# A hybrid decoder step: the order of weight splits and probabilities, and a low-rank gate block with both weight parts

## What is computed

```python
h = rms_norm(x, norm_g)
proj = h @ w_in                       # 13,840 columns, split into twelve parts
q = rope(rms_norm(a_q, q_norm_g), pos)        # 16 heads of 64
k = rope(rms_norm(a_k, k_norm_g), pos)        # 4 heads
# A: attention in a window of 128 keys, with a sink per head
m = max(max(s), sink); p = exp(s - m); p = p / (sum(p) + exp(sink - m)); o_a = p @ v
# B: trailing means over 2, 4, 8 and 16 positions, minus the token, times w_pool
# C: gated linear attention; its decay comes from a low-rank gate:
log_a = log_sigmoid(c_lr @ w_gate_lr + b_gate) / 16      # c_lr is (tokens, 16)
br = branches * silu(gate paths), each @ w_branch
y = x + (sum over branches of sigmoid(gates) * br) @ w_out
```

## Time and profile before

| what | value |
|---|---|
| median of three runs (lowest to highest) | 2330.77 us (2329.85 to 2331.12) |
| the profiled execution's own time | 2328.41 us |
| span of the profile | 2326.6 us |
| TensorE busy | 2292.4 us (99%), 15984 matmuls |
| VectorE, ScalarE, GpSimd busy | 1373.4 us (59%), 1013.4 us (44%), 71.6 us (3%) |
| mean granted TensorE clock | 0.998 |
| read from and written to HBM | 341.59 and 20.50 MB |

### The profile page before, as it was taken

One profiled execution on the slowest core, in us unless ns is written; L12 is line 12 of the kernel. 1 busy time (PEld: TensorE's weight loads), 2 busy tenths in 40 slices (PEclk: granted clock), 3 DMA queues, 4 the chain that ended last, 5 costly groups with the idle time before them and its releaser, 6 DMA issues.

```text
span 2326.6 us, 38299 instructions
## 1 busy us (share of the span) xinstructions
PE 2292.4 (99%) x15984; PEld 2248.5 (97%) x15984; DVE 1373.4 (59%) x2335; ACT 1013.4 (44%) x1816; POOL 71.6 (3%) x110
## 2 busy tenths in 40 slices
PE   8999999999999999999999999999999999999997
PEld 8999999899999999999999999988999999999997
DVE  6766866865554455446657677578654445544543
ACT  5444356654333333333343443566543333333332
POOL 0010000000000000000001001000000000000000
PEclk9999999999999999999999999999999999999999
DMA  7333653334444444445553436533344444444453
GB/s 271 134 131 130 220 203 121 100 118 150 149 152 148 154 146 153 147 154 191 193 205 126 144 129 235 179 116 103 122 150 151 148 151 149 153 147 153 158 197 118
DMA packets 97132, 360.65 MB, mean 155 GB/s; under 512 B 11376, under 2 KB 11376, under 8 KB 96128
## 3 DMA queue, kind: packets, MB, share of 16 engines
q1 hardware_dynamic: 86400, 313.82, 40.2%
q0 software_dynamic: 9840, 43.02, 5.2%
q10 hardware_dynamic: 720, 1.36, 0.2%
HBM read 341.59 MB, written 20.50 MB: 156 GB/s over the span
## 4 chain that ended last, share of the span: by engine, by line
PE 90%; DVE 5%; ACT 3%; issue 2%; DMA 0%; POOL 0%; ACTq 0%; DVEq 0%; POOLq 0%
PE main L1491 83%; PE side L1491 5%; DVE w_lo L428 1%; ACT tc L1256 1%; PE side L1495 1%; ACT w_hi L1049 1%; ACT probs L1216 0%; DVE small L767 0%; DVE q_a L443 0%; ACT tb L1068 0%; DVE probs L762 0%; DVE tc L443 0%; DVE ta L447 0%; ACT tb L1070 0%; DVE q_a L739 0%
## 5 line engine op out<-in xcount | busy, mean ns | idle before, releaser
L1491 PE MATMUL main<-xg_hi,w_hi 128*128 128x320 f32 x3488 | 1093.7, 314 | 10.1 <-DVE w_lo L428 10.1
L428 DVE TENSOR_TENSOR w_lo<-raw,w_hi 128x512 fp32r<-128x512 f32 x1192 | 790.6, 697 | 521.0 <-ACT w_hi L1049 509.4
L1491 PE MATMUL main<-xg_hi,w_lo 128*128 128x320 f32 x3488 | 1078.5, 309 | 0.0
L1491 PE MATMUL main<-xg_lo,w_hi 128*128 128x320 f32 x3488 | 1078.3, 309 | 0.0
L1049 ACT ACTIVATE w_hi<-raw 128x512 fp32r<-128x512 f32 x1192 | 714.5, 626 | 702.2 <-PE main L1491 687.7
L1491 PEld LDWEIGHTS main<-xg_hi,w_hi 128*128 128x128 f32 x3488 | 655.6, 188 | 19.2 <-DVE xg_lo L462 10.1
L1491 PEld LDWEIGHTS main<-xg_lo,w_hi 128*128 128x128 f32 x3488 | 655.7, 188 | 2.0
L1491 PEld LDWEIGHTS main<-xg_hi,w_lo 128*128 128x128 f32 x3488 | 655.4, 188 | 0.0
L1491 PE MATMUL main<-branch_hi,w_hi 128*128 128x320 f32 x768 | 237.3, 309 | 0.0
L1491 PE MATMUL main<-branch_lo,w_hi 128*128 128x320 f32 x768 | 237.3, 309 | 0.0
L1491 PE MATMUL main<-branch_hi,w_lo 128*128 128x320 f32 x768 | 237.3, 309 | 0.0
(11 more groups left out here) (226 smaller groups left out, 1320.6 us busy)
## 6 DMA issues: line engine op xcount, KB each, us to landing
raw<-in_w_stream SPq DMA_DIRECT2D x596, 512.0 KB, 3.3
state<-in_state POOLq DMA_DIRECT2D x16, 512.0 KB, 6.4
out_state_s<-state POOLq DMA_DIRECT2D x16, 512.0 KB, 3.0
w_pool<-in_w_pool POOLq DMA_DIRECT2D x2, 1024.0 KB, 8.2
cache_k<-in_cache_k POOLq DMA_DIRECT2D x2, 1024.0 KB, 5.5
cache_v<-in_cache_v POOLq DMA_DIRECT2D x2, 1024.0 KB, 7.9
out_k_window<-in_cache_k_tok POOLq DMA_DIRECT2D x2, 960.0 KB, 10.0
out_new_v_s<-in_cache_v_tok POOLq DMA_DIRECT2D x2, 960.0 KB, 11.3
```

The lines of the kernel that those rows point to most:

```text
L428: dve.tensor_tensor(w_lo[Q % RAWS][:, half], raw[Q % RAWS][:, half], w_hi[Q % HIS][:, half].bitcast(F32), ALU.subtract).then_inc(lo_ready, 1)
L1491: return pe.matmul(out, lhsT, rhs, start=start, stop=stop)
```

## The change

It has four parts.

1. **The low-rank blocks.** VectorE writes the low part of the 16 real columns into columns 16 to 31 of the same piece of `w_hi`, instead of the whole low part into `raw`. TensorE then multiplies the piece, with both parts in it, by the high and by the low activations (`rank_products`): two products for a piece instead of three. Rows 0 to 15 of the result come from the high weights and 16 to 31 from the low ones. The gate's own product is made over 32 rows, with the small matrix `w_gate` loaded twice, one copy under the other, so that both are summed. (This adds the product of the low parts, which was left out before.)
2. **The probabilities** are normalised in the beat of their scores, after the masking and the low part of b+3, and before `vector_part`. The table `PROBS_AT` goes.
3. **ScalarE's splits.** `split_hi_to(Q + 3)` is done in every beat ahead of `scalar_part` (in layer 0 only from beat 5 on).
4. **Ahead of that split** now stand, in `level_exps`, the exponentials of the linear attention's levels, and in `between_beats`, the gate copies and the swap of the heads' halves. In beats with scores `between_beats` stays behind the answers to the steps, where it was.

```diff
-PROBS_AT = {}
...
@@ split_lo @@
+                    if LR_AT <= Q % BEATS < LR_AT + LR_BEATS:
+                        hi = w_hi[Q % HIS][:, half].rearrange("p (k c) -> p k c", k=4)
+                        low = raw[Q % RAWS][:, half].rearrange("p (k c) -> p k c", k=4)
+                        dve.tensor_tensor(hi[:, :, RANK:2 * RANK], low[:, :, 0:RANK],
+                                          hi[:, :, 0:RANK].bitcast(F32), ALU.subtract).then_inc(lo_ready, 1)
+                        continue
@@ vector_probs @@
-                for name, k in PROBS_AT.get(beat, ()):
+                for name, k, _ in STEPS.get(beat, ()):
@@ VectorE's beat @@
-                    vector_probs(l, beat)
                     split_lo_to(Q + 2)
-                    vector_softmax(l, beat)
                     if scored_at(beat):
+                        vector_softmax(l, beat)
                         split_lo_to(Q + 3)
+                        vector_probs(l, beat)
                     vector_part(l, beat)
@@ ScalarE: new functions, taken out of scalar_part @@
+            def level_exps(l, beat):
...
+            def between_beats(l, beat):
+                for g in gated_at(beat, 1):
+                    gate_high(l, g)
+                for name, k, _ in STEPS.get(beat - 1, ()):
+                    if name in ("k_norm", "q_norm"):
+                        vec("normed", l, (name, k))
...
@@ in scalar_part, behind the answers to the steps @@
-                for g in gated_at(beat, 1):
-                    gate_high(l, g)
...
+                if scored_at(beat):
+                    between_beats(l, beat)
@@ ScalarE's beat @@
                     split_hi_to(Q + 2)
-                    if scored_at(beat):
+                    level_exps(l, beat)
+                    if not scored_at(beat):
+                        between_beats(l, beat)
+                    if l or beat > RMS_BEAT:
                         split_hi_to(Q + 3)
                     scalar_part(l, beat)
@@ GpSimd @@
-            load(w_gate[0:RANK, :], ins["w_gate"][0], w_gate_in)
+            for i in range(2):
+                load(w_gate[RANK * i:RANK * i + RANK, :], ins["w_gate"][0], w_gate_in)
@@ TensorE @@
+            def rank_products(Q, G, k0, first, last):
+                out = main[:, 2 * (G % 2), 0:TOK]
+                for s in range(2):
+                    pe.wait_ge(lo_ready, Q * 2 + (s + 1))
+                    for kk in range(4):
+                        k, c = k0 + 4 * s + kk, 512 * s + P * kk
+                        both = w_hi[Q % HIS][:, c:c + P]
+                        mm(out, both, xg_hi[:, k, :], first and s == 0 and kk == 0, False)
+                        ins_ = mm(out, both, xg_lo[:, k, :], False, last and s == 1 and kk == 3)
+                    ins_.then_inc(half_used, 1)
...
-                        last = mm(side[:, h, 0:TOK], w_gate[0:RANK, DK * h:DK * h + DK], ta[0:RANK, 0, :])
+                        last = mm(side[:, h, 0:TOK], w_gate[0:2 * RANK, DK * h:DK * h + DK], ta[0:2 * RANK, 0, :])
...
-                        block_products(Q, G, 1, xg_hi, xg_lo, 8 * part, part == 0, part == 1, narrow=True)
+                        rank_products(Q, G, 8 * part, part == 0, part == 1)
```

More of the change, by code:

```diff
@@ L142 @@
 N_STEPS = len(ORDER)
-PROBS_AT = {}
-for _b in sorted(STEPS):
-    for _n, _k, _ in STEPS[_b]:
-        if _n.endswith("p_turn"):
-            PROBS_AT.setdefault(_b - 1, []).append((_n.replace("p_turn", "scores"), _k))
 TAKE = {g: first_beat(g) + 3 for g in range(N_IN)}
@@ L1131, in gate_take @@
                     gate_high(l, g)
+            def level_exps(l, beat):
+                for k in range(1, 8):
+                    if beat == 17 + 2 * k:
+                        B = LEVELS[k - 1]
+                        e4, n = segs(lev_e, B)
+                        vec("level_gap", l, k)
+                        a(act.activation(e4[:, :, :, 0:B], e4[:, :, :, 0:B], ACT.Exp, scale=-1.0))
+                        act.activation(e4[:, :, :, B:2 * B], e4[:, :, :, B:2 * B], ACT.Exp).then_inc(level_exp, 1)
+            def between_beats(l, beat):
[4 more added lines that the diff above has]
+                        vec("normed", l, (name, k))
+                        for q in range(4):
+                            ins = act.activation(tc[32 * q:32 * q + 32, :, :], ta[32 * (q ^ 1):32 * (q ^ 1) + 32, :, :],
+                                                 ACT.Copy)
+                            if q == 3:
+                                ins.then_inc(swapped, 1)
+                            else:
+                                a(ins)
             def scalar_part(l, beat):
@@ L1274, in scalar_part @@
                     last.then_inc(stack_hi, 1)
-                for k in range(1, 8):
-                    if beat == 17 + 2 * k:
-                        B = LEVELS[k - 1]
-                        e4, n = segs(lev_e, B)
-                        vec("level_gap", l, k)
-                        a(act.activation(e4[:, :, :, 0:B], e4[:, :, :, 0:B], ACT.Exp, scale=-1.0))
-                        act.activation(e4[:, :, :, B:2 * B], e4[:, :, :, B:2 * B], ACT.Exp).then_inc(level_exp, 1)
                 if beat == 34:
@@ L1372, in _ @@
                     pool.wait_ge(half_used, last_half(l - 1, IN_BEATS + MIX_BEATS - 1))
-                if l:
-                    load(w_gate[0:RANK, :], ins["w_gate"][l], w_gate_in)
+                for i in range(2 if l else 0):
+                    load(w_gate[RANK * i:RANK * i + RANK, :], ins["w_gate"][l], w_gate_in)
                 load(w_pool[:, :, :], ins["w_pool"][l], w_pool_in)
@@ L1495, in turn, with block_products @@
                 return pe.transpose(out, src, ident[0:src.shape[0], 0:src.shape[0]])
-            def block_products(Q, G, tiles, hi, lo, k0, first, last, narrow=False):
+            def rank_products(Q, G, k0, first, last):
[8 more added lines that the diff above has]
+                    ins_.then_inc(half_used, 1)
+            def block_products(Q, G, tiles, hi, lo, k0, first, last):
                 base = 2 * (G % 2)
@@ L1502, in block_products @@
                     pe.wait_ge(lo_ready, Q * 2 + (s + 1))
-                    nk = 4 if narrow else 2
-                    w = 128 if narrow else 256
-                    for kk in range(nk):
-                        k = k0 + nk * s + kk
+                    for kk in range(2):
+                        k = k0 + 2 * s + kk
                         for t in range(tiles):
-                            c = 512 * s + kk * w + t * P
+                            c = 512 * s + kk * 256 + t * P
                             out = main[:, base + t, 0:TOK]
                             st = first and s == 0 and kk == 0
-                            sp_ = last and s == 1 and kk == nk - 1
+                            sp_ = last and s == 1 and kk == 1
                             mm(out, wh[:, c:c + P], hi[:, k, :], st, False)
```

12 lines of the change are left out of this document (1 added, 11 removed).

## The result

The changed kernel takes 2334.84 us (median of 16 runs, 2333.73 to 2335.34), the kernel before 2330.46 on the same chip (2329.82 to 2331.51): a ratio of 1.0018, 95% interval [1.0011, 1.0025]. It is slower by 4.4 us; the forecast was 8 us faster, and the range ended at 2326.2. The span of the profiled execution is 2332.3 us (before: 2326.6). The difference of the two spans, 5.7 us, is larger than that of the medians, since the traced execution of the kernel before lies 2.05 us under its median (2328.41) and that of the changed kernel 0.7 us under (2334.14).

The account below looks back on a forecast made before the run. TensorE bounds the kernel: the number of matmuls times their pitch, plus its waits. The terms -4.69 - 0.6 - 1.3 + 0.55 - 2.3 = -8.3 us took the median from 2330.77 to 2322.5 us, range 2318.5 to 2326.2.

Parts of the forecast that it names:

- Part 1: Low-rank blocks, beats 8 and 9 of both layers: 32 matmuls fewer at 0.1467 us, -4.69 us.
- beat 13: Both layers: the wait for weights and the long first row go, as ScalarE splits block 13 earlier; -0.6 us.
- `k_turn`: Both layers: its wait of 0.64 us goes, as the keys are ready 1.4 us earlier; -1.3 us.
- Block 7 of layer 1: Beat 4: its split ahead of the norm's inverse root makes TensorE wait; +0.55 us, bounds 0 and +2.
- The chain on ScalarE: Attention steps 1 and 2: 9.9 us from masking's end to the copy's end, 0.7 us late for the values, twice.
- Step 4. Division before the gate product, not after: Attention beats: 0.3 of the transposes' 1.57 us wait stays, -1.3; values 4 and transposes 5 then wait, +0.9.
- After that the chain of VectorE and ScalarE runs with the slack that it had less 1.4, and nothing waits: Attention beats after the waits foreseen at steps 4 and 5: slack shrinks by 1.4 us, no further wait.
- parts 2 to 4: Attention beats: one wait given for another, -1.3 us in layer 0, -1.0 in layer 1; -2.3 us in all.
- C: Rival: in six attention beats the values wait 4.1 us each for swap and split; +7.1, 2337.9 us; chance 0.04.
- A: Rival: the attention beats give nothing, everything else holds; -6.0, 2324.8 us; chance 0.25.
- B: Rival: ScalarE's copies come in time and TensorE keeps its lead in all steps; -17.5, 2313.3 us; chance 0.06.
- D: Rival: TensorE waits in or behind beats 8 to 10 for a block; only -3.5, 2327.3 us; chance 0.10.

Follow-up runs that it names:

- e1: The changed kernel with both engines' orders as before, so the low-rank blocks alone: 2323.72 us, ratio 0.9975.
- e3: The changed kernel with the division a beat later as before; low-rank blocks and ScalarE's new orders (parts 3 and 4) kept: 2321.93 us, ratio 0.9967.
- e9: e8 with no split ahead by ScalarE in beats 47 and 48, where it copies into v_stack: 2313.33 us, ratio 0.9927.
- e8: e3 with ScalarE copying the turned probabilities ahead of the swap and the split in beats 84, 88 and 92: 2315.98 us, ratio 0.9939.
- e5: The changed kernel with VectorE's gate product ahead of the early division in beats with scores: 2322.54 us, ratio 0.9968.
- e2: The changed kernel with ScalarE's order as before; low-rank blocks and the early division kept: 2330.30 us, ratio 1.0001.
- e4: The changed kernel with ScalarE's copies first and no split ahead in beats without scores that hold a copy: 2328.39 us, ratio 0.9993.
- e6: e3 with step 4 alone divided in the beat of its scores, ahead of a gate product: 2328.74 us, ratio 0.9995.
- e12: The changed kernel with the reorderings of e5, e8 and e9, and layer 1's inverse root ahead of block 7's split: 2314.96 us, ratio 0.9935.
- e11: e9 with layer 1's inverse root ahead of block 7's split, and step 3 alone divided in its scores' beat: 2313.60 us, ratio 0.9931.
- e7: The changed kernel with the transposes of step 4 made three times, 24 more in all: 2331.35 us, ratio 1.0007.

## Why the prediction was wrong, by its steps

**Right.** Part 1 (-4.7, e1 alone too), beat 13 and `k_turn`. Block 7 of layer 1 cost 0.7 us against 0.55, by the mechanism foreseen, but the closeness is luck: in the traces of e3 to e9, with the same order at this place, it is 0.34 to 1.60. In the attention beats the waits of the values of steps 0 to 2 were 1.74, 1.07 and 1.06 us where 1.6, 0.7 and 0.7 were forecast, and the transposes of steps 0 to 3 no longer wait. The chain on ScalarE held, and e8 shows that its links were the right ones: the swap and the split ahead of the copy. Its length was added up wrongly: the prediction's own walk goes from 369.8 to 380.2, 10.4 us and not 9.9, and 10.4 is what the changed kernel's step 0 shows (367.6 to 378.0). The half us accounts for most of what steps 1 and 2 wait beyond the forecast. The values of step 3 waited 1.43 us where 1.1 was forecast.

**Wrong: "Step 4. Division before the gate product, not after"**, with the product and the gate copy "0.9 us later than before". The step treated the two as changing places. They do not: before, the product lay in the time in which VectorE would else wait for ScalarE's exponentials. Put behind the division it leaves that time empty: it comes later by the 1.92 us that VectorE is idle and the 1.45 us of the division. That is 3.4 us, counted from the low part of block 98, against e3 and against the kernel before. Counted from the end of TensorE's block 97, which is the time that the waits are made of, the product ends 1.76 us behind it in the changed kernel, 0.03 ahead of it before and 2.23 ahead of it in e3: 1.8 us later than before, not 0.9, although the low part now comes 1.7 us earlier. The copy of the values of step 3 starts 2.8 us later than before by the same count, since one split (1.04 us) now stands ahead of it too. The rows to see this by were in the trace of before: the exponentials take 1.9 us on ScalarE, and what VectorE did meanwhile was the work now put last.

**Wrong: "After that the chain of VectorE and ScalarE runs with the slack that it had less 1.4, and nothing waits".** This was said and not walked through (the 0.9 us foreseen just before it, at the values of step 4 and the transposes of step 5, did not come either). The late product goes by ScalarE's high part and one split to the copy of the values of step 3, and by the PSUM banks to the scores of step 5 (2.90 + 0.16 us) and again to those of step 7 (1.24). I had listed who waits for the turned probabilities and not who waits for the banks. In both layers that is 8.6 us, and with the 2.0 us of the lower clock in block 98 it makes most of the difference of 11.2 us between forecast and trace in these beats. e5 takes it back by moving the product alone, and its attention beats come to -2.4 us, the forecast's -2.3; that the two agree so closely is partly luck, since steps 0 to 2 came out 0.5 us a layer worse than foreseen.

**Wrong: no word on beat 52 (+2.6).** For every beat I asked whether ScalarE had been late with a high part, and so what an early split frees. I asked what it delays only in layer 1's beat 4. But a split for b+3 waits until TensorE has used block b, so it holds back whatever of ScalarE's beat stands behind it. e9 takes the 2.6 us back.

**Credited to the wrong part.** The text put the gains at steps 0 to 2 under "parts 2 to 4" together. e2, e3 and e8 show that part 3 makes them and part 2 nothing: at these steps the division was the next instruction of VectorE in any case. By that, part 2 had little to gain but at steps 3 and 4, and it was the only part that lost.

**The rivals.** None of them was this case. C had the right sign and the wrong place: the waits of the values at steps 0 to 2 stayed at 1.1 to 1.7 us, well under its 2.9. A was the nearest for steps 0 to 2: gains and new waits there come to +0.7 in layer 0. B is out by the same waits, and D too: behind beats 8 and 9 TensorE has no gap, and behind beat 10 the same 2.44 us of a side step as before.

## What to carry to other kernels

When an instruction is moved ahead of another on an in-order engine, look at what the engine was waiting for at that place: work that stood in the shadow of another engine's operation delays all behind it once it is put after the wait: here by the idle time and the division, 3.4 us for 1.7 us of work. Starting a ring's next item early makes the engine wait for the ring's slot, so look for everything of that beat that is behind it, and follow each late item to all that it frees, buffers and banks too. And walk the chain on until it meets slack that a row shows; "after that nothing waits" is a term like any other.

## What the runs showed of the hardware that was not expected

A break of TensorE of 2.8 to 5.5 us between two blocks, with side steps in it, can cost more than itself. The granted clock behind it was 0.53 in layer 0 of the changed kernel (440 to 443 us) and 0.50 in layer 1 (1594 to 1597 us), and in the traces where it fell (changed, e2, e4, e6, e12) the next block took 0.7 to 1.6 us more. It does not always do so: gaps of 3.76 us in both layers of e4, and of 4.27 and 4.26 us in e6, ended with the clock up in one layer and down in the other, and a wait of 1.83 us for the values of step 3 left it at 1.00 in e11 and brought it down in e12. What tells these apart was not tried. Transposes made twice more in the gap (e7) kept the clock up in both layers and made the kernel faster while it did more.
